# Value products of cached keys in a hybrid decoder step: three split passes with the probabilities stationary, or one fp32 pass with the values stationary

## The chip, the cores and the metric

The kernel runs on one core of one Trainium2 chip. The metric is the device time of one execution in microseconds, lower is better. Three runs of the kernel before took 2503.12 to 2511.63 us, median 2504.29 us.

## What is computed

One layer of a decoder for 512 prompt tokens and 8 x 8 sample tokens (8 sequences, 8 new tokens each) that share the weights. One projection gives queries, keys and values of 3 dilation groups x 8 heads x 128, gates, and the halves of a gated MLP. The part that the change touches is the attention of the sample tokens, over cached and over new keys:

```
kg = k_all[:, idx].astype(jnp.float32)
vg = v_all[:, idx].astype(jnp.float32)
s = jnp.einsum('bthe,btjhe->bthj', q.astype(jnp.float32), kg) * (dh ** -0.5)
s = jnp.where(valid[None, :, None, :], s, -jnp.inf)
m = jnp.max(s, axis=-1, keepdims=True)
p = jnp.exp(s - m)
den = jnp.sum(p, axis=-1)
o = jnp.einsum('bthj,btjhe->bthe', p, vg) / den[..., None]
```

The three groups' outputs are merged by their softmax denominators, which the kernel does by one softmax over all keys of all three groups. The result is multiplied by silu(z_B) and goes, with the MLP branch, through three more products and a layer norm.

## The kernel before, in words

All large products run in three passes: an operand is rounded to fp32r (the high part, ACT, L942), the rest is a second fp32r operand (the low part, VectorE, L1231, the helper low), and TensorE adds high x high, low x high and high x low.

The program has four stages: the projections of the heads (L682), then eight frames, one per head, then two products of the branches, then the output product with the layer norm. The frames run from about 1231 to 2018 us. In a frame TensorE works through 64 parts of the gates' projection (L736, six matmuls of 128x288 a part, a quarter of weights for every four parts) and between the parts does one head's attention. The order is written out by hand: 40 steps, and part_of(f, step) says behind which part a step comes (8 parts to 5 steps; in frame 1, where the attention starts later, part 16 and then 6 to 5). TensorE, ACT and VectorE each walk the same list of parts and steps, so a step's place is the same on all three, and they meet by semaphores alone.

The steps: early sample scores, four rounds of prompt scores (L792, L794), masking with maximum (L1444), exponential (L1124), normalising (L1441), turning the probabilities with transposes (L756) and prompt outputs (L804). The scores of the cached keys of two groups are made by VectorE in eight pieces, far_ones (L1419, L1420), two of them already for the next head at steps 34 and 38. At step 27 the sample probabilities are turned, and ACT copies them spread out into psh (7 tiles of 64 columns: 8 sequences x 8 tokens for each tile of 128 cached keys); VectorE makes psl, the low part.

Then come the eight value products, one per sequence b, at steps 30 to 37 (SLOT_PVS). Each needs the value tile of its sequence: 128 keys by 7 x 128 values (448 KB), which POOL's queue loads to one of four slots of cache (L559). ACT rounds it to vh (round_values, steps 24 to 36), VectorE makes vl. cached_out(b) on TensorE (L819) has the 8 probability columns of the sequence as the stationary operand and the values as the moving one, 7 tiles x 3 passes, and puts 8 rows x 128 columns to the score banks scp. At step 39 VectorE copies the 8 x 1024 results to osm (L1535); sample_out on TensorE adds up the new keys' part (L826) and turns osm back by eight transposes (L829); VectorE adds the two and multiplies by silu(z_B) in zt (L1537, L1538, L1540). That last step signals y_done.

The queues: POOL issues, in this order from a frame's end, the store of y (store_y, waits for y_done, L610), the value tiles 0 to 3 of the next head (each waits for pv_used of the product four before), the four loads of the head after it (load_head, L519 to L526), then key tiles ones 4 and 5 (L543). SP loads the gate weights (L396) and stores the gates (L403). The scores' banks are passed on by score_read, the turned probabilities' by turn_read.

Of the kernel before, what the change touches and what calls it, by code (L numbers as in the profile page):

```python
# [12 lines left out]
P = 128  # L13
# [79 lines left out]
def slot_pv(i):  # L93
# [6 lines left out]
SLOT_VS = [24, 26, 31, 32, 33, 34, 35, 36]  # L100
# [7 lines left out]
          ("pv", 2), "far", ("pv", 3), "cached_pv", "sample_out"]  # L108
N_SC = len(SCORES)
SIGNALLED = [n for n in SCORES if n != "cached_pv"]  # L110
# [28 lines left out]
def build(nc, x_t, x_res, near_k, ones_k, units_k, cache_v, w_in, bias_t, w_st, w8_t, b_s, ln_v_g, ln_v_b, w_o_a, w_o_b,  # L139
# [11 lines left out]
    with ExitStack() as ctx:  # L151
# [56 lines left out]
        far_1, far_2, otmp = put("far_1", 4, SAMP), put("far_2", SAMP), put("otmp", SAMP)  # L208
# [10 lines left out]
        place_v = R2 + 2304  # L219
        cache = put("cache", 4, 7, P)  # L220
        vl = sb("vl", [P, 4, 7, P], place_v, F32R)
# [4 lines left out]
        place_s = place_v + (28 + 56) * P * 4  # L226
        vh = [put("vh0", 7, P, dt=F32R), put("vh1", 7, P, dt=F32R)]
        sc = sb("sc", [P, 6 * P], place_s)
        pt = sb("pt", [P, 6 * P], place_s + CACHED * 4)
        place_m = place_s + 2 * CACHED * 4  # L230
        ss, psl = put("ss", KEYS + NEW), put("psl", 7 * SAMP + 4, dt=F32R)
        osm = sb("osm", [DEC_T, 8 * P], place_m)
        psh, mask = put("psh", 7 * SAMP + 4, dt=F32R), put("mask", 9 * P)
# [53 lines left out]
        ps_round, ps_zero = sem("ps_round"), sem("ps_zero")  # L287
# [4 lines left out]
        v_round, v_split, ps_split, pv_used = sem("v_round"), sem("v_split"), sem("ps_split"), sem("pv_used")  # L292
        biased, expd, normed = sem("biased"), sem("expd"), sem("normed")
        y_done, y_stored, vector_done = sem("y_done"), sem("y_stored"), sem("vector_done")
# [50 lines left out]
        def _(sp):  # L345
# [75 lines left out]
            def load_gate(n, g):  # L421

                if n >= 4:
                    sp.wait_ge(merged, n - 3)
                elif n == 0:
                    sp.wait_ge(y_done, HEADS)
                sp.wait_ge(g_stored, 16 * (g + 1))
                sp.dma_start(gbuf[:, n % 4, :], gate_d[g]).then_inc(gate_in[n % 4], 16)
# [28 lines left out]
        def _(pool):  # L457
# [150 lines left out]
            def store_y(h):  # L608
                pool.wait_ge(y_done, h + 1)
                pool.dma_start(yb_d[h], zt[h % 2]).then_inc(y_stored, 16)  # L610
            frames(frame)

            pool.wait_ge(y_done, HEADS)
# [46 lines left out]
        def _(pe):  # L660
# [84 lines left out]
            def turn_blocks(f, name, pairs_):  # L745

                n = TURN_NAMES.index(name)
                if n % 2 == 0:
                    if is_at(f, 1) and n == 0:
                        pe.wait_ge(item_read, ITEMS_ALL)  # L750
                    else:
                        pe.wait_ge(turn_read, N_TURN * (f - 1) + n)
                    if name == ("pt", 0, 0) and not is_at(f, 1):
                        pe.wait_ge(ps_split, 3 * (f - 1))
                for cols, src, rows, width in pairs_:
                    done = pe.transpose(turn[0:width, n % 2, cols:cols + rows], src, ident[0:rows, 0:rows])  # L756
                done.then_inc(turned, 1)

            def frame(f, par):
# [48 lines left out]
                def cached_out(b):  # L808
                    if b == 0:
                        bank_free("cached_pv")  # L810

                        pe.wait_ge(ps_split, 3 * f)

                    pe.wait_ge(v_split, 8 * (f - 1) + b + 1)
                    for n in range(7):
                        hi, lo = vh[b % 2][:, n, :], vl[:, b % 4, n, :]
                        at = n * SAMP + DEC_T * b
                        for t, (p, val) in enumerate(((psh, hi), (psh, lo), (psl, hi))):
                            done = pe.matmul(scp[0:DEC_T, b * P:(b + 1) * P], p[:, at:at + DEC_T], val,  # L819
                                             start=(n == 0 and t == 0), stop=(n == 6 and t == 2))  # L820
                    done.then_inc(pv_used, 1)

                def sample_out():
                    bank_free("sample_out")
                    for g in range(GROUPS):
                        pe.matmul(scp[:, SEQ:SEQ + SAMP], vN[par][g][0:SAMP, 4, :], psn[0:SAMP, g, :],  # L826
                                  start=(g == 0), stop=(g == GROUPS - 1))
                    for b in range(DEC_B):
                        done = pe.transpose(scp[:, DEC_T * b:DEC_T * (b + 1)], osm[:, b * P:(b + 1) * P],  # L829
                                            ident[0:DEC_T, 0:DEC_T])  # L830
                    done.then_inc(scored, 1)

                for part in range(PARTS):
# [11 lines left out]
                    for s in range(STEPS):  # L845
# [28 lines left out]
                        if s == 39:  # L874
                            sample_out()
# [65 lines left out]
        def _(act):  # L941
# [129 lines left out]
            def frame(f, par):  # L1071
                def turn_out(name):
# [10 lines left out]
                    elif name == ("pts", 0):  # L1083
                        probs = turn[:, bank, :]
                        copy(psh[:, 0:SAMP], probs[:, 0:SAMP]).then_inc(ps_round, 1)
                        copy(by_class(psh), probs[:, SAMP:2 * SAMP].rearrange("p (k c) -> p c k", c=4)
                             ).then_inc(ps_round, 1)
                        out = by_unit(psh)
                        src = probs[:, 2 * SAMP:3 * SAMP].rearrange("p (b u r) -> p u b r", u=2, r=4)
                    else:  # L1090
                        out, src = psn[0:SAMP], turn[0:SAMP, bank, 0:NEW].rearrange("p (n c) -> p n c", n=GROUPS)
                    copy(out, src).then_inc(turn_read, 1)

                def round_values(b):

                    slot = b % 4

                    act.wait_ge(v_in[slot], 16 * (2 * (f - 1) + b // 4 + 1))

                    if b == 0:  # L1100
                        act.wait_ge(turned, turn_no(f, ("pt", 3, 1)))
                    elif b == 1:
                        act.wait_ge(scored, signal_no(f, ("pv", 3)))
                    else:
                        act.wait_ge(pv_used, 8 * (f - 1) + b - 1)
                    copy(vh[b % 2][:], cache[:, slot, :, :]).then_inc(v_round, 1)

                for part in range(PARTS):
# [6 lines left out]
                    for s in range(STEPS):  # L1115
# [15 lines left out]
                        for b in range(DEC_B):  # L1131
                            if s == SLOT_VS[b]:
                                round_values(b)
# [5 lines left out]
            def branch_slot(t):  # L1139

                ahead(Q_B + t)
                if t == 0:
# [5 lines left out]
                    act.wait_ge(y_done, HEADS)  # L1148
# [60 lines left out]
        def _(dve):  # L1209
# [191 lines left out]
            def frame(f, par):  # L1401
# [44 lines left out]
                for part in range(PARTS):  # L1446
# [11 lines left out]
                    for s in range(STEPS):  # L1458
# [8 lines left out]
                        if s == SLOT_EARLY + 1:  # L1467
                            if f == 1:
                                dve.wait_ge(consts, 48)
                                for n_ in range(2):  # L1470
                                    dve.wait_ge(v_stored[n_], 16 * (VA_PAIRS + (2 - n_) * HEADS))
                                v.memset(psh[:].bitcast(F32), 0.0).then_inc(zeroed, 1)
# [35 lines left out]
                        if s == SLOT_FAR + 3:  # L1508
                            dve.wait_ge(expd, 5 * f)
                            normalise(ss[0:SAMP], SAMP, 5)  # L1510
                            v.memset(psl[:].bitcast(F32), 0.0).then_inc(ps_zero, 1)
                        if s == SLOT_PTS + 1:

                            b0 = TURN_NAMES.index(("pts", 0)) % 2
                            dve.wait_ge(turn_read, turn_no(f, ("pts", 1)))
                            dve.wait_ge(ps_round, 2 * f)
                            dve.wait_ge(ps_zero, f)
                            probs = turn[:, b0, :]
                            low(psl[:, 0:SAMP], probs[:, 0:SAMP], psh[:, 0:SAMP]).then_inc(ps_split, 1)
                            low(by_class(psl), probs[:, SAMP:2 * SAMP].rearrange("p (k c) -> p c k", c=4),  # L1520
                                by_class(psh)).then_inc(ps_split, 1)
                            low(by_unit(psl), probs[:, 2 * SAMP:3 * SAMP].rearrange("p (b u r) -> p u b r", u=2, r=4),
                                by_unit(psh)).then_inc(ps_split, 1)
                        for b in range(DEC_B):
                            if s == SLOT_VS[b]:

                                dve.wait_ge(v_round, 8 * (f - 1) + b + 1)
                                low(vl[:, b % 4, :, :], cache[:, b % 4, :, :], vh[b % 2][:]).then_inc(v_split, 1)
# [291 lines left out]
```

## Time and profile before

| | |
|---|---|
| median of 3 runs | 2504.29 us (2503.12 to 2511.63) |
| profiled execution, own time | 2510.55 us |
| its span, first to last instruction | 2508.9 us |
| mean granted TensorE clock | 0.965 |
| TensorE busy | 2306.7 us, 92%, 17744 records |
| VectorE busy | 1611.3 us, 64% |
| ACT busy | 923.8 us, 37% |
| POOL busy | 265.0 us, 11% |
| HBM traffic | 142 GB/s over the span |

The profile is of one execution. A matmul's end is modelled and matmuls are pipelined, so the time that one takes in a row of them is read from the distance of the starts, not from its duration. A plain fp32 matmul (and no transpose) stands in the trace as two records, each with a weight load. PE is TensorE's matmuls, PEld its weight loads. PEclk is the share of 2.4 GHz that was granted. In a matmul's row the first pair, as 128*8, is rows and columns of the stationary operand, the second, as 128x128, rows and columns of the moving one.

### The profile page before, as it was taken

To read this page: it belongs to the slowest core of one execution; us is meant where nothing else is said; L and a number is where in the kernel's file an instruction comes from. 1 tells how busy PE (TensorE), PEld (TensorE's weight loads), DVE (VectorE), ACT (ScalarE), POOL (GpSimd) and SP (SyncE) were. 2 spreads that over 40 slices of the span, in tenths; PEclk is the share of its full clock that TensorE was granted. 3 is DMA by queue.
4 is the path that set the end of the run, shared out by engine and by line. 5 is a ranking of instruction groups with operands and counts; after the bars stand their busy time and mean duration, and the time that the engine had idled before them with its cause. 6 is when DMAs were issued, how large, how long until landed. Compare 5 with 4: busy or idle time off the path is not lost.

```text
span 2508.9 us, 44550 instructions
## 1 busy us (share of the span) xinstructions
PE 2306.7 (92%) x17744; PEld 2258.8 (90%) x17744; DVE 1611.3 (64%) x2085; ACT 923.8 (37%) x1326; POOL 265.0 (11%) x453
## 2 busy tenths in 40 slices
PE   5999999999999999999968978979889979999993
PEld 4999999999999999999957978978779879999993
DVE  7677877777778777787565655655565647553336
ACT  4544444444444444444322322322323333332221
POOL 0100000000000000000222121122121110000003
PEclk8999999999999999999988999989999989999996
DMA  4433443343334333443576566566666563344332
GB/s 145 135 117 117 119 132 100 118 122 115 112 118 130 110 112 118 131 123 118 174 231 207 147 217 201 163 194 192 171 203 179 153 191 119 123 123 146 101 106 89
DMA packets 400348, 358.94 MB, mean 143 GB/s; under 512 B 15664, under 2 KB 359744, under 8 KB 398368
## 3 DMA queue, kind: packets, MB, share of 16 engines
q1 hardware_dynamic: 363168, 206.28, 28.2%
q0 software_dynamic: 36992, 149.90, 18.2%
q8 instruction: 150, 2.46, 0.4%
q14 instruction: 38, 0.31, 0.0%
HBM read 309.74 MB, written 46.37 MB: 142 GB/s over the span
## 4 chain that ended last, share of the span: by engine, by line
PE 76%; DVE 10%; DMA 7%; issue 3%; ACT 1%; POOL 1%; SPq 0%; DVEq 0%; ACTq 0%; POOLq 0%
PE acc L682 46%; PE acc L736 23%; DMA ones<-in_ones_k 4%; DVE prod L1419 2%; DVE far L1420 2%; PE scp L819 2%; PE scp L792 1%; PE turn L756 1%; DMA cache<-in_cache_v 1%; DVE sc L1444 1%; PE turn L691 1%; DMA gbuf<-gate_rows 1%; ACT wh L942 1%; DVE wl L1231 1%; DVE sc L1441 1%
## 5 line engine op out<-in xcount | busy, mean ns | idle before, releaser
L682 PE MATMUL acc<-xh,wph 128*128 128x288 f32 x2912 | 868.3, 298 | 38.4 <-DVE wpl L1231 29.2
L682 PE MATMUL acc<-xl,wph 128*128 128x288 f32 x2912 | 860.3, 295 | 0.0
L682 PE MATMUL acc<-xh,wpl 128*128 128x288 f32 x2912 | 857.2, 294 | 0.0
L682 PEld LDWEIGHTS acc<-xh,wph 128*128 128x128 f32 x2912 | 547.0, 188 | 40.9 <-issue 23.2
L682 PEld LDWEIGHTS acc<-xh,wpl 128*128 128x128 f32 x2912 | 549.5, 189 | 0.0
L682 PEld LDWEIGHTS acc<-xl,wph 128*128 128x128 f32 x2912 | 548.1, 188 | 0.0
L1231 DVE TENSOR_TENSOR wl<-raw,wh 128x512 fp32r<-128x512 f32 x256 | 176.8, 691 | 417.2 <-ACT wh L942 416.6
L942 ACT ACTIVATE wh<-raw 128x512 fp32r<-128x512 f32 x256 | 161.0, 630 | 565.6 <-PE acc L736 463.5
L736 PE MATMUL acc<-xh,wh 128*128 128x288 f32 x1024 | 237.7, 314 | 8.9 <-DVE wl L1231 6.1
L736 PE MATMUL acc<-xl,wh 128*128 128x288 f32 x1024 | 224.4, 301 | 0.0
L736 PE MATMUL acc<-xh,wl 128*128 128x288 f32 x1024 | 223.9, 301 | 0.0
L1022 ACT ACTIVATE s<-acc,bias 128x288 f32<-128x288 f32 x208 | 98.7, 500 | 273.8 <-PE acc L682 249.5
L1231 DVE TENSOR_TENSOR wpl<-w_a,wph 128x1024 fp32r<-128x1024 f32 x104 | 127.4, 1225 | 83.1 <-ACT wph L942 81.5
L736 PEld LDWEIGHTS acc<-xh,wh 128*128 128x128 f32 x1024 | 166.5, 195 | 12.5 <-DVE wl L1231 6.5
L1231 DVE TENSOR_TENSOR wpl<-w_c,wph 128x1024 fp32r<-128x1024 f32 x104 | 127.2, 1223 | 73.5 <-ACT wph L942 72.8
L736 PEld LDWEIGHTS acc<-xl,wh 128*128 128x128 f32 x1024 | 169.6, 194 | 0.0
L942 ACT ACTIVATE wph<-w_a 128x1024 fp32r<-128x1024 f32 x104 | 110.1, 1059 | 160.4 <-DVE w_a L1254 160.4
L736 PEld LDWEIGHTS acc<-xh,wl 128*128 128x128 f32 x1024 | 169.2, 194 | 0.0
L942 ACT ACTIVATE wph<-w_c 128x1024 fp32r<-128x1024 f32 x104 | 109.8, 1056 | 66.3 <-PE acc L682 63.8
L736 PE MATMUL acc<-mh,wh 128*128 128x288 f32 x512 | 110.8, 298 | 0.0
L736 PE MATMUL acc<-mh,wl 128*128 128x288 f32 x512 | 109.7, 296 | 0.0
L736 PE MATMUL acc<-ml,wh 128*128 128x288 f32 x512 | 109.5, 295 | 0.0
(212 smaller groups left out, 3637.4 us busy)
## 6 DMA issues: line engine op xcount, KB each, us to landing
raw<-in_w_in SPq DMA_DIRECT2D x128, 256.0 KB, 5.0
cache<-in_cache_v POOLq DMA_DIRECT2D x64, 448.0 KB, 5.3
w_a<-in_w_in SPq DMA_DIRECT2D x52, 512.0 KB, 3.8
w_c<-in_w_in SPq DMA_DIRECT2D x52, 512.0 KB, 3.8
w_b<-in_w_in SPq DMA_DIRECT2D x52, 512.0 KB, 3.8
w_d<-in_w_in SPq DMA_DIRECT2D x52, 512.0 KB, 3.9
ones<-in_ones_k POOLq DMA_DIRECT2D x64, 256.0 KB, 3.2
raw<-in_w_out SPq DMA_DIRECT2D x64, 256.0 KB, 2.7
```

Of the source, the lines that this page charges most:

```text
L682: done = pe.matmul(bank, w[ring][:, k, :], a[x][:, k, :], start=(j in (0, 1, 3, 5) and k == 0 and t == 0), stop=(k == HK - 1 and t == 2), ...
L691: done = pe.transpose(turn[0:rows, b, c * P:(c + 1) * P], src, ident[:])
L736: done = pe.matmul(accv[p][:, h, :], w[:, q % RING, n, :], moving(k, h, low), start=(first and n == 0 and t == 0), stop=(last and n == QB ...
L756: done = pe.transpose(turn[0:width, n % 2, cols:cols + rows], src, ident[0:rows, 0:rows])
L792: pe.matmul(scp[:, 0:SEQ], qT[par][0][:, cols], kT[par][0][:, 0:SEQ], start=True, stop=True)
L819: done = pe.matmul(scp[0:DEC_T, b * P:(b + 1) * P], p[:, at:at + DEC_T], val, start=(n == 0 and t == 0), stop=(n == 6 and t == 2))
L942: copy = lambda out, src: nc.scalar.activation(out, src, ACT.Copy)
L1022: nc.scalar.activation(out[:], bank_x, ACT.Identity, bias=b, scale=sign).then_inc(s_copied, 1)
L1231: return v.tensor_tensor(out, src, hi.bitcast(F32), ALU.subtract)
L1419: links.then(v.tensor_tensor(prod[:], keys, rows.broadcast_to([P, 4, 2, P]), ALU.mult))
L1420: v.tensor_reduce(far_1[:, :, DEC_T * b:DEC_T * b + DEC_T], prod[:].rearrange("p j u (c d) -> p j (u c) d", d=32), mybir.AxisListType.X, A ...
L1441: v.tensor_scalar(tile, tile, small[0:rows, c + 1:c + 2], None, ALU.mult).then_inc(normed, 1)
```

## The change

The value product is done in plain fp32 in one pass, with the value tile stationary (128 keys x 128 values) and the 8 probability columns moving, so that its result comes out with the values on the partitions, as the new keys' part does. It is added to that part in the same columns of the bank: the three products of the new keys (before L826) go ahead of product 0 and open the bank, and the 56 products of cached values add to it. Gone are the rounding and splitting of values (vh, vl), the splitting of probabilities (psl with its memset), osm, the eight transposes, sample_out as a step of its own, otmp and two of VectorE's three last operations. VectorE multiplies straight from the bank; it signals score_read, which takes the place of y_done everywhere. The step lists, the loads and the 64 parts are the same.

```diff
-SLOT_VS = [24, 26, 31, 32, 33, 34, 35, 36]
 SCORES = ["early", ("qk", 0), ("qk", 1), ("pv", 0), ("qk", 2), ("pv", 1), ("qk", 3),
-          ("pv", 2), "far", ("pv", 3), "cached_pv", "sample_out"]
+          ("pv", 2), "far", ("pv", 3), "sample_out"]
...
-        vh = [put("vh0", 7, P, dt=F32R), put("vh1", 7, P, dt=F32R)]
-        sc = sb("sc", [P, 6 * P], place_s)
-        pt = sb("pt", [P, 6 * P], place_s + CACHED * 4)
...
+        sc, pt = put("sc", 6 * P), put("pt", 6 * P)
+        ss, ps = put("ss", KEYS + NEW), put("ps", 7 * SAMP + 4)
...
             def store_y(h):
-                pool.wait_ge(y_done, h + 1)
+                pool.wait_ge(score_read, N_SC * (h + 1))
...
                 def cached_out(b):
                     if b == 0:
-                        bank_free("cached_pv")
-                        pe.wait_ge(ps_split, 3 * f)
-                    pe.wait_ge(v_split, 8 * (f - 1) + b + 1)
+                        bank_free("sample_out")
+                        pe.wait_ge(ps_spread, 2 * f)
+                        pe.wait_ge(turn_read, turn_no(f, ("pts", 1)))
+                        for g in range(GROUPS):
+                            pe.matmul(scp[:, SEQ:SEQ + SAMP], vN[par][g][0:SAMP, 4, :], psn[0:SAMP, g, :],
+                                      start=(g == 0), stop=False, skip_group_check=True)
+                    pe.wait_ge(v_in[b % 4], 16 * (2 * (f - 1) + b // 4 + 1))
                     for n in range(7):
-                        hi, lo = vh[b % 2][:, n, :], vl[:, b % 4, n, :]
                         at = n * SAMP + DEC_T * b
-                        for t, (p, val) in enumerate(((psh, hi), (psh, lo), (psl, hi))):
-                            done = pe.matmul(scp[0:DEC_T, b * P:(b + 1) * P], p[:, at:at + DEC_T], val,
-                                             start=(n == 0 and t == 0), stop=(n == 6 and t == 2))
+                        done = pe.matmul(scp[:, SEQ + DEC_T * b:SEQ + DEC_T * (b + 1)], cache[:, b % 4, n, :],
+                                         ps[:, at:at + DEC_T], start=False, stop=(n == 6), skip_group_check=True)
                     done.then_inc(pv_used, 1)
-
-                def sample_out():
-                    bank_free("sample_out")
-                    for g in range(GROUPS):
-                        pe.matmul(scp[:, SEQ:SEQ + SAMP], vN[par][g][0:SAMP, 4, :], psn[0:SAMP, g, :],
-                                  start=(g == 0), stop=(g == GROUPS - 1))
-                    for b in range(DEC_B):
-                        done = pe.transpose(scp[:, DEC_T * b:DEC_T * (b + 1)], osm[:, b * P:(b + 1) * P],
-                                            ident[0:DEC_T, 0:DEC_T])
-                    done.then_inc(scored, 1)
...
-                def round_values(b):
-                    slot = b % 4
-                    act.wait_ge(v_in[slot], 16 * (2 * (f - 1) + b // 4 + 1))
...
-                    copy(vh[b % 2][:], cache[:, slot, :, :]).then_inc(v_round, 1)
...
-                            v.memset(psl[:].bitcast(F32), 0.0).then_inc(ps_zero, 1)
...
-                                low(vl[:, b % 4, :, :], cache[:, b % 4, :, :], vh[b % 2][:]).then_inc(v_split, 1)
...
                         if s == 39:
                             dve.wait_ge(pv_used, 8 * f)
-                            v.tensor_copy(osm[:], scp[0:DEC_T, :]).then_inc(score_read, 1)
-                            dve.wait_ge(scored, signal_no(f, "sample_out"))
-                            links.then(v.tensor_copy(otmp[:], scp[:, SEQ:SEQ + SAMP]))
-                            v.tensor_tensor(otmp[:], otmp[:], scp[:, 0:SAMP], ALU.add).then_inc(score_read, 1)
-                            dve.wait_ge(score_read, score_no(f, "sample_out"))
-                            v.tensor_tensor(zt[par][:, SEQ:TOK], otmp[:], zt[par][:, SEQ:TOK], ALU.mult).then_inc(y_done, 1)
+                            v.tensor_tensor(zt[par][:, SEQ:TOK], scp[:, SEQ:SEQ + SAMP], zt[par][:, SEQ:TOK],
+                                            ALU.mult).then_inc(score_read, 1)
```

On TensorE in frame 2, from the last part ahead of product 0. Before, a product was 21 rows with the 8 probability columns stationary, of which the first four stand here (a matmul's size in these rows is that of its result):

```order
L736 MATMUL acc<-xh_52,wl 128x288
L736 MATMUL acc<-xh_55,wl 128x288
L819 MATMUL scp<-vh_120,psh 8x128 [waits v_split,ps_split,score_read]
L819 MATMUL scp<-vl,psh 8x128
L819 MATMUL scp<-vh_120,psl 8x128
L819 MATMUL scp<-vh_120,psh 8x128
```

Now (L728 is the old L736, L804 the old L826):

```order
L728 MATMUL acc<-xh_52,wl 128x288
L728 MATMUL acc<-xh_55,wl 128x288
L804 MATMUL scp<-psn,qkv 128x64 [waits turn_read,ps_spread,score_read]
L804 MATMUL scp<-psn,qkv 128x64 x2
L810 MATMUL scp<-ps,cache 128x8 [waits v_in0]
L810 MATMUL scp<-ps,cache 128x8 x6
L728 MATMUL acc<-xh_52,wh 128x288
```

The new keys' products have moved from behind part 62 to here, a product has 7 rows, and its first one waits for the transfer of its value tile.

On VectorE at the end of frame 2, before:

```order
L1405 COPY qz<-qkv 128x8x8 [waits head_in0,scored]
L1231 TENSOR_TENSOR wl<-raw,wh 128x512 [waits w_round]
L1419 TENSOR_TENSOR prod<-ones,qb 128x1024 [waits ones_sum,ones_in1]
L1420 TENSOR_REDUCE far_105<-prod 128x4x8 [waits vector_done]
L1535 COPY osm<-scp 8x1024 [waits pv_used]
L1537 COPY otmp<-scp 128x64 [waits scored]
L1538 TENSOR_TENSOR otmp<-otmp,scp 128x64 [waits vector_done]
L1540 TENSOR_TENSOR qkv<-otmp,qkv 128x64 [waits score_read]
```

And now (line numbers are lower by 38 and more):

```order
L1367 COPY qz<-qkv 128x8x8 [waits head_in0,scored]
L1193 TENSOR_TENSOR wl<-raw,wh 128x512 [waits w_round]
L1381 TENSOR_TENSOR prod<-ones,qb 128x1024 [waits ones_sum,ones_in1]
L1382 TENSOR_REDUCE far_105<-prod 128x4x8 [waits vector_done]
L1479 TENSOR_TENSOR qkv<-scp,qkv 128x64 [waits pv_used]
```

Four operations with a wait for TensorE between them have become one, which waits for the last value product.

## Rows read from the trace of the kernel before

**Rows 1.** The page, part 1: busy time of the engines

```profile
PE 2306.7 (92%) x17744; PEld 2258.8 (90%) x17744; DVE 1611.3 (64%) x2085; ACT 923.8 (37%) x1326; POOL 265.0 (11%) x453
```

**Rows 2.** TensorE's waits, 1230 to 2025 us: total us, times, longest us

```profile
PE turn L756 <- DVE sc L1441: 72.4, 21, 11.4
...
PE scp L826 <- DVE osm L1535: 8.5, 7, 1.3
```

**Rows 3.** The chain of waits, 1437 to 1471 us: start us, us, what

```profile
1438.70 0.64 ACT wh L942
...
1439.97 1.23 DVE prod L1419
...
1442.45 1.13 DVE osm L1535
...
1445.63 0.24 DVE qkv L1540
...
1451.97 15.04 DMA ones<-in_ones_k
```

**Rows 4.** Timeline of PE: products 0 and 7 of frame 2, and TensorE's restart

```profile
1419.89 0.22 PE L819 MATMUL scp<-vh,psh 128*8 128x128 f32 x1
...
1438.44 0.22 PE L819 MATMUL scp<-vh,psh 128*8 128x128 f32 x1
...
1470.30 1.12 PE L756 MATMUL turn<-ident,sc 128*128 128x128 f32 x4 [10.14 <-DVE sc L1441]
```

**Rows 5.** Timeline of PE: product 0 of frame 1 and the part behind it

```profile
1325.59 0.23 PE L819 MATMUL scp<-vh,psh 128*8 128x128 f32 x1
...
1326.85 0.48 PE L736 MATMUL acc<-xh,wh 128*128 128x288 f32 x2
1327.17 0.43 PE L736 MATMUL acc<-xl,wh 128*128 128x288 f32 x2
1327.44 0.43 PE L736 MATMUL acc<-xh,wl 128*128 128x288 f32 x2
```

**Rows 6.** Tile vh: count, ns least/median/most, first and last start

```profile
L819 PE MATMUL scp<-vh,psh x448: 218/223/227, 1325.6 to 2013.6; 128*8 128x128 f32 x150
...
L942 ACT ACTIVATE vh<-cache x64: 935/952/957, 1317.8 to 2009.0; 128x896 fp32r<-128x896 f32 x64
L1231 DVE TENSOR_TENSOR vl<-cache,vh x64: 1018/1092/1094, 1318.8 to 2010.0; 128x896 fp32r<-128x896 f32 x64
```

**Rows 7.** Timeline of PEld: weight loads, last one's duration 0.19, 0.14, 0.14 us

```profile
1443.62 0.74 PEld L826 LDWEIGHTS scp<-psn,qkv 64*128 64x128 f32 x6 [1.55 <-DVE osm L1535]
1444.42 0.56 PEld L829 LDWEIGHTS scp<-ident,osm 8*128 8x128 f32 x8
...
1314.67 0.54 PEld L784 LDWEIGHTS scp<-sums,far 128*64 128x64 f32 x8 [0.16 <-issue]
```

**Rows 8.** Timeline of PEld at half clock; the last load of three took 0.34 us

```profile
1375.21 0.76 PEld L794 LDWEIGHTS scp<-qkv 128*128 128x128 f32 x3 [0.52 <-issue]
...
1376.31 0.57 PEld L736 LDWEIGHTS acc<-xl,wh 128*128 128x128 f32 x2
1376.79 0.57 PEld L736 LDWEIGHTS acc<-xh,wl 128*128 128x128 f32 x2
```

**Rows 9.** The chain of waits, 1300 to 1500 us: a value tile

```profile
1421.61 6.27 DMA cache<-in_cache_v
```

**Rows 10.** Stretches: us, busy us (records) by engine, PEclk, DMA share, GB/s

```profile
1344.00:1347.40 3.40, 2.80 (x25) 2.48 (x24) 1.81 (x4) 0.00 (x0) 0.54 (x1) 1.00 0.29 77
1347.50:1350.90 3.40, 3.40 (x16) 3.40 (x16) 2.06 (x4) 1.26 (x2) 2.79 (x6) 0.50 0.53 131
1351.00:1354.30 3.30, 3.30 (x28) 3.14 (x28) 2.03 (x3) 0.63 (x1) 3.15 (x5) 1.00 0.87 275
...
1419.80:1439.80 20.00, 19.68 (x237) 18.97 (x237) 11.41 (x13) 8.33 (x11) 2.74 (x5) 1.00 0.54 174
...
1299.70:1306.40 6.70, 3.19 (x21) 2.40 (x20) 6.34 (x9) 1.55 (x4) 1.31 (x3) 1.00 0.53 164
```

More of the change, by code:

```diff
@@ L107 @@
 SCORES = ["early", ("qk", 0), ("qk", 1), ("pv", 0), ("qk", 2), ("pv", 1), ("qk", 3),
-          ("pv", 2), "far", ("pv", 3), "cached_pv", "sample_out"]
+          ("pv", 2), "far", ("pv", 3), "sample_out"]
 N_SC = len(SCORES)
-SIGNALLED = [n for n in SCORES if n != "cached_pv"]
+SIGNALLED = [n for n in SCORES if n != "sample_out"]
 N_SIG = len(SIGNALLED)
@@ L207, in build @@
         qz = put("qz", TOK)
-        far_1, far_2, otmp = put("far_1", 4, SAMP), put("far_2", SAMP), put("otmp", SAMP)
+        far_1, far_2 = put("far_1", 4, SAMP), put("far_2", SAMP)
         psn, smask, sums = put("psn", GROUPS, SAMP), put("smask", KEYS + NEW), put("sums", P)
@@ L218, in build @@
         gstage = put("gstage", TOK)
-        place_v = R2 + 2304
         cache = put("cache", 4, 7, P)
-        vl = sb("vl", [P, 4, 7, P], place_v, F32R)
         near = put("near", DEC_B * P)
@@ L225, in build @@
         ones, prod = put("ones", 2, 4 * P), put("prod", 4, 2, P)
-        place_s = place_v + (28 + 56) * P * 4
-        vh = [put("vh0", 7, P, dt=F32R), put("vh1", 7, P, dt=F32R)]
-        sc = sb("sc", [P, 6 * P], place_s)
-        pt = sb("pt", [P, 6 * P], place_s + CACHED * 4)
[L230 to L233, printed above, removed]
+        sc, pt = put("sc", 6 * P), put("pt", 6 * P)
+        ss, ps = put("ss", KEYS + NEW), put("ps", 7 * SAMP + 4)
+        mask = put("mask", 9 * P)
         m = sb("m", [P, KB, TOK], FREE)
@@ L286, in build @@
         ones_sum, units_sum, far_ready = sem("ones_sum"), sem("units_sum"), sem("far_ready")
-        ps_round, ps_zero = sem("ps_round"), sem("ps_zero")
+        ps_spread = sem("ps_spread")
         q_spread, zeroed = sem("q_spread"), sem("zeroed")
@@ L291, in build @@
         v_in = [sem(f"v_in{i}") for i in range(4)]
-        v_round, v_split, ps_split, pv_used = sem("v_round"), sem("v_split"), sem("ps_split"), sem("pv_used")
+        pv_used = sem("pv_used")
         biased, expd, normed = sem("biased"), sem("expd"), sem("normed")
-        y_done, y_stored, vector_done = sem("y_done"), sem("y_stored"), sem("vector_done")
+        y_stored, vector_done = sem("y_stored"), sem("vector_done")
         yb_in, yb_round, yb_split = sem("yb_in"), sem("yb_round"), sem("yb_split")
@@ L425, in load_gate @@
                 elif n == 0:
-                    sp.wait_ge(y_done, HEADS)
+                    sp.wait_ge(score_read, N_SC * HEADS)
                 sp.wait_ge(g_stored, 16 * (g + 1))
@@ L608, in store_y @@
             def store_y(h):
-                pool.wait_ge(y_done, h + 1)
+                pool.wait_ge(score_read, N_SC * (h + 1))
                 pool.dma_start(yb_d[h], zt[h % 2]).then_inc(y_stored, 16)
             frames(frame)
-            pool.wait_ge(y_done, HEADS)
+            pool.wait_ge(score_read, N_SC * HEADS)
             pool.dma_start(vn[:].rearrange("p c (g d) -> p c g d", g=HEADS),
@@ L752, in turn_blocks @@
                         pe.wait_ge(turn_read, N_TURN * (f - 1) + n)
-                    if name == ("pt", 0, 0) and not is_at(f, 1):
-                        pe.wait_ge(ps_split, 3 * (f - 1))
                 for cols, src, rows, width in pairs_:
@@ L873, in frame @@
                                 cached_out(b)
-                        if s == 39:
-                            sample_out()
             frames(frame)
@@ L1084, in turn_out @@
                         probs = turn[:, bank, :]
[L1085 to L1088, printed above, removed]
+                        copy(ps[:, 0:SAMP], probs[:, 0:SAMP]).then_inc(ps_spread, 1)
+                        copy(by_class(ps), probs[:, SAMP:2 * SAMP].rearrange("p (k c) -> p c k", c=4)
+                             ).then_inc(ps_spread, 1)
+                        out = by_unit(ps)
                         src = probs[:, 2 * SAMP:3 * SAMP].rearrange("p (b u r) -> p u b r", u=2, r=4)
@@ L1092, in turn_out @@
                     copy(out, src).then_inc(turn_read, 1)
-                def round_values(b):
-                    slot = b % 4
-                    act.wait_ge(v_in[slot], 16 * (2 * (f - 1) + b // 4 + 1))
[L1100 to L1105, printed above, removed]
-                    copy(vh[b % 2][:], cache[:, slot, :, :]).then_inc(v_round, 1)
                 for part in range(PARTS):
@@ L1130, in frame @@
                                                  accum_out=small[0:SAMP, 5:6]).then_inc(expd, 1)
-                        for b in range(DEC_B):
-                            if s == SLOT_VS[b]:
-                                round_values(b)
             frames(frame)
@@ L1147, in branch_slot @@
                     round_yb(6, 7, yb_raw[:, 6:7, :])
-                    act.wait_ge(y_done, HEADS)
+                    act.wait_ge(score_read, N_SC * HEADS)
                     round_yb(7, 8, zt[1].rearrange("p (o t) -> p o t", o=1))
@@ L1471, in frame @@
                                     dve.wait_ge(v_stored[n_], 16 * (VA_PAIRS + (2 - n_) * HEADS))
-                                v.memset(psh[:].bitcast(F32), 0.0).then_inc(zeroed, 1)
+                                v.memset(ps[:], 0.0).then_inc(zeroed, 1)
                             dve.wait_ge(scored, signal_no(f, "early"))
@@ L1510, in frame @@
                             normalise(ss[0:SAMP], SAMP, 5)
-                            v.memset(psl[:].bitcast(F32), 0.0).then_inc(ps_zero, 1)
[L1512 to L1527, printed above, removed]
-                                low(vl[:, b % 4, :, :], cache[:, b % 4, :, :], vh[b % 2][:]).then_inc(v_split, 1)
                         if s == 37 and f < HEADS:
```

## The prediction, made before the change was run

> **What bounds the kernel now.** I read the page first: TensorE is busy 92% of the span, every other engine far less [rows 1]. That says where to look, not what the end waits for. The waits of TensorE inside the eight frames (1230 to 2025 us) show two that repeat: 72.4 us in 21 waits for the normalised scores, and 8.5 us in 7 for the copy osm [rows 2]. The chain of waits around the end of frame 2 explains both [rows 3]. ACT's rounding starts at 1438.70, when part 59 of the frame has been multiplied. VectorE then forms two key products (1439.97 to 1442.45), copies osm, TensorE turns it back, and VectorE's last product (L1540) ends at 1445.87. Only then does POOL's queue store y and issue the next head's loads; the key tile behind them is on the way for 15.04 us. TensorE, which had work up to about 1460.2, stands idle for 10.14 us until 1470.30 [rows 4]. So a frame is a ring: y done, 24.4 us of queue, transfer and VectorE, then TensorE's parts 12 to 59, then the tail to the next y. TensorE's time counts between its restart and part 59; between y and the restart it has 10 us to spare.
>
> **The value products now.** A product is 21 matmuls of one weight load each: 1325.59 to 1326.85, 1.26 us, or 60 ns per matmul; big matmuls between them are 0.27 us apart for two, 0.133 each, and a part has six [rows 5]. In frame 2, product 0 starts at 1419.89 and product 7 at 1438.44 [rows 4]: 7 products (8.82) and 11 parts (11 x 0.80 = 8.80) make 17.62 us, and 0.9 us are waits. All 64 products are 3 x 448 matmuls [rows 6], 1344 x 0.060 = 81 us.
>
> **The new product, at full clock.** It has 7 plain fp32 matmuls with 128 value columns stationary and 8 columns moving. A plain fp32 matmul shows as two records, each with a load. The trace has no 128-wide load with 8 fp32 columns behind it, so I bound its price:
> - Nearest row: L826, a plain fp32 product, 128 stationary columns, 64 moving. Six loads take 0.74 us with one load's 0.19 us at the end, so they are (0.74 - 0.19) / 5 = 0.110 us apart [rows 7]. L784, 64 stationary and 32 moving: (0.54 - 0.14) / 7 = 0.057. Half the stationary columns, half the time: the load sets it.
> - Lower bound: the turns L829, also 128 stationary and 8 moving, (0.56 - 0.14) / 7 = 0.060 us [rows 7]. But these are transposes, another mode, with one record each.
> - Upper bound: the load at half clock, (0.76 - 0.34) / 2 = 0.21 us [rows 8].
>
> I take 0.110, because L826 is the same operation with the same load. A product becomes 14 x 0.110 = 1.54 us, 0.28 more than now. The Trainium skill, page "TensorE: Matmul & The Clock Gate", section "LDWEIGHTS (loading the stationary operand)", speaks against this change: the time of a load goes with its columns. Eight columns were loaded before and 128 now; by its formula a load of 128 is an estimated 107 ns, and the sum would be 0.04 us a product lower. The trace agrees in the pair L826 and L784.
>
> **The sum at full clock, per frame.** Up to product 7's start: seven products cost 7 x 0.28 = +1.96; the three sample products (L826) move ahead of product 0, 6 x 0.11 = +0.67; the waits there for ACT and VectorE (0.9 us in frame 2, 0.3 to 0.8 in the others, 0.5 taken) go: **+2.1 us**. The tail: part 59 ends where product 7 starts, 1438.44. VectorE's rounding and two key products stay, to 1442.45, and the one multiplication of 0.23 us follows; product 7 has ended by 1440.0 plus, so it is no wait. y is done at 1442.7 in place of 1445.87: **-3.2 us**. Together -1.1 us for frames 2 to 7; frame 1, with 8 parts instead of 11 in the stretch, about the same, a little more. In frame 8 nothing waits for y alone, but for TensorE's last part, which loses its idle 1.3 us and the eight turns but keeps the +2.1, so about +0.6. Sum: **about -7 us**, under the 0.5% (12.5 us) that a measurement of this kernel can tell from no change.
>
> **What costs or brings nothing.** ACT loses 64 copies of 0.95 us and VectorE 64 differences of 1.09 [rows 6], next to three small splits, a memset and the osm copies. They lay beside TensorE's products, and both engines wait in this stretch already, so beyond the 0.5 us above nothing comes of them. The psh copies keep their place as ps. POOL's loads wait on the same counters as before. TensorE now waits for the value tile itself: tile 4 is asked for at product 0's end and lands 6.27 us later [rows 9], 1428.9 in frame 2's terms, while product 4 is due at about 1431.5; 2.6 us to spare.
>
> **The clock.** This decides. While the old products run, the granted clock is 1.00 throughout: TensorE streams 128 columns every 60 ns, from 1419.80 to 1439.80 [rows 10]. Where did it fall? In the 3.4 us from 1344.00 TensorE was busy 2.80 us, with 25 records, 14 of them the L826 products and the 8-column turns, and the next 3.4 us ran at 0.50, that is 1.2 of 2.4 GHz. From 1299.70 it was busy only 3.19 of 6.70 us, all with long matmuls, and stayed at 1.00 [rows 10]. So short matmuls behind wide loads did not hold the clock as the long ones did, though they looked busy. The new products are of this kind: 16 columns' streaming (two records of 8) per 0.22 us of loading. Between them stand one or two parts of dense matmuls. Where two products are one part apart (steps 30/31, 32/33, 35/36) some 3.9 us hold little but loads; with two parts between them it is denser. I therefore expect three falls in each of frames 2 to 8 and five in frame 1, whose products are nearly all one part apart: 26. A fall that is not followed by a long idle lasts 3.4 us in the trace (1347.50 to 1350.90; 1.00 again after [rows 10]). In it the big matmuls take 0.24 us in place of 0.133 (0.48 for two) and loads 0.21 in place of 0.11 [rows 8], so 3.4 us do the work of 1.8: each costs 1.6 us. 26 x 1.6 = **+42 us**. All lie before part 59, on the ring. After it, a slow clock only eats the 10 us of slack.
>
> The Trainium skill (same page, Part 1, "The HAM clock gate") says the clock is released by activity and falls back without it; taken as matmul-issuing time this would keep the clock up here, and the sum would stop at -7 us. The row of 1344.00 is against that reading, so it is a rival below.
>
> **Total:** -7 + 42 = +35 us. The profiled execution took 2510.6 us, 6.3 over the median of the runs; the difference is applied to the median: 2504.3 + 35 = **2539 us**. Bounds of the clock's cost: 0, and the whole stretch at half clock.
>
> **Rivals.**
> - *The clock holds* (loads count as work): -7 us, 2497. For it: TensorE is never idle in the stretch, and in the 3.4 us before the fall at 1347.50 it was idle for 0.6. Against it: 1344.00. Chance 0.20.
> - *Faster, the other side: the load goes at the turns' pace*, 0.060 us instead of 0.110, in L810 of the change. Then a product takes 0.84 us, -0.42; a stretch 7 x -0.42 + 0.67 - 0.5 = -2.8, the tail -3.2, so -6.0 in seven frames and -4 in the last: -46 us, 2458. It decides from a spacing below about 0.085 us, where a product is cheaper than the old 1.26. For: same load width, same 8 moving columns. Against: L826. Chance 0.08.
> - *The clock stays at half from product 0 to part 59*, because one dense part between products does not bring it back. The stretch of 0.67 + 10.8 + 8.8 = 20.3 us takes 1.3 + 7 x 3.0 + 11 x 1.44 = 38 us: +18 a frame, +144 - 7 = +137, 2641. For: after the stall at 1470 it needs dense work to return. Against: two-part gaps are over half dense. Chance 0.10.
> - *Value tiles land late*: some 1 to 2 us a frame on top, 2550. Chance 0.05.
> - My forecast: 0.57, with 2515 to 2590 as its own range.
>
> **The numbers.** Range 2494 to 2590: it leaves out the fast load and the full half clock. Faster by over 0.5% takes the fast load and the low edge of the first rival: 0.12. Within 0.5%: the rest of that rival and a few falls only: 0.22. Slower: 0.66.
>
> **What would show it.** L810: 896 records about 0.110 us apart at full clock and 0.21 at half; product 0 to product 7 20.3 us where the clock is 1.00 throughout; half-clock stretches of 3.4 us inside the product stretches; VectorE's single product about 4.2 us after product 7's start; no wait for osm; the 24.4 us from y to TensorE's restart unchanged. A spacing of 0.06, or a clock of 1.00 in all eight stretches, would prove the forecast wrong.

## The result, and the profile after

The changed kernel takes 2588.65 us (median of 4 runs, 2568.40 to 2600.82) against 2506.67 before (4 runs): a ratio of 1.032, 95% interval 1.025 to 1.039. It is slower, by 82 us, where 35 were forecast. The time lies 1.4 us under the upper edge of the range (2590), and two of the four executions lie above that edge, so it is luck that the median fell inside. The profiled execution took 2590.81 us, against 2510.55 before.

The page of the changed kernel, part 1, to be read beside [rows 1]:

```profile
PE 2400.2 (93%) x17232; PEld 2357.0 (91%) x17232; DVE 1522.9 (59%) x1965; ACT 864.5 (33%) x1262; POOL 264.1 (10%) x453
```

TensorE has 512 records fewer and is busy 94 us longer. ACT and VectorE have lost 59 and 88 us of work; the end did not come sooner for it. TensorE's waits, as in [rows 2]:

```profile
PE turn L746 <- DVE sc L1403: 69.1, 21, 9.8
```

The wait for osm is gone; the large one, for the normalised scores after each frame's start, has kept its size. No wait for a value tile is in the list. So the 82 us are not a wait: TensorE works through the frames more slowly. The timeline of PEld in frame 3 shows how:

```profile
1538.02 1.75 PEld L810 LDWEIGHTS scp<-ps,cache 128*128 128x128 f32 x14
1539.65 0.55 PEld L728 LDWEIGHTS acc<-xh,wh 128*128 128x128 f32 x2
...
1541.07 3.13 PEld L810 LDWEIGHTS scp<-ps,cache 128*128 128x128 f32 x14
```

A product of 14 loads takes 1.6 us at full clock and 3.0 at half; the clock fell at the end of the first one. Big matmuls start 0.24 us apart (0.48 for two). The price of a load is 0.112 us from start to start at full clock and 0.213 at half (medians over the records of all 64 products at that clock): the forecast had 0.110 and 0.21.

The stretches from product 0 to product 7's start, all eight frames; the columns are those of [rows 10], PEclk is the last but two:

```profile
1328.90:1359.40 30.50, 30.50 (x147) 30.50 (x147) 6.19 (x7) 1.26 (x2) 2.73 (x5) 0.54 0.29 87
1436.50:1460.80 24.30, 24.30 (x165) 24.30 (x165) 3.84 (x5) 1.26 (x2) 2.72 (x5) 0.79 0.47 142
1538.00:1570.60 32.60, 32.60 (x165) 32.58 (x165) 3.84 (x5) 1.26 (x2) 2.72 (x5) 0.58 0.34 106
1648.50:1676.10 27.60, 27.60 (x165) 27.57 (x165) 3.84 (x5) 1.26 (x2) 2.72 (x5) 0.69 0.40 125
1753.10:1785.70 32.60, 32.60 (x165) 32.60 (x165) 3.84 (x5) 1.26 (x2) 2.72 (x5) 0.57 0.35 106
1863.40:1890.90 27.50, 27.50 (x166) 27.50 (x166) 3.84 (x5) 1.26 (x2) 2.72 (x5) 0.69 0.41 126
1968.10:2000.80 32.70, 32.70 (x167) 32.66 (x166) 3.84 (x5) 1.26 (x2) 2.72 (x5) 0.57 0.34 106
2071.20:2095.40 24.20, 24.20 (x166) 24.20 (x166) 1.38 (x2) 1.26 (x2) 2.19 (x4) 0.80 0.45 132
```

Together 232.0 us, where the kernel before took 143.2 for the same eight (16.3 to 18.6 each, at 1.00 throughout). A mean clock of 0.57 over 32.6 us means 2 x (1 - 0.57) x 32.6 = 28 us at half clock. In all it is 165 us. Below, a "fall" is a piece of time at half clock. In frames 1, 3, 5 and 7 the clock fell with the first product or two and stayed down almost to the last: one fall of 34.1 us in frame 1, which runs on past product 7, and of 23.9 us in the others. In the even frames it rose in between: frames 2 and 8 have three falls of 3.4 us each, frames 4 and 6 have one of 10.2 us among them. Two pieces of frame 2 and one of frame 3, in the same columns:

```profile
1440.60:1443.80 3.20, 3.20 (x15) 3.20 (x15) 0.00 (x0) 0.09 (x1) 0.55 (x1) 0.50 0.72 220
1444.10:1447.20 3.10, 3.10 (x29) 3.10 (x28) 2.80 (x3) 0.24 (x1) 0.54 (x1) 1.00 0.36 109
1539.60:1563.30 23.70, 23.70 (x106) 23.70 (x106) 3.49 (x4) 1.26 (x2) 2.72 (x5) 0.50 0.39 122
```

The account closes on starts of instructions. Product 7 of frame 8 starts at 2012.56 before and at 2095.36 now, +82.8 us. Of it +3.3 lie ahead of frame 1's product 0, +88.8 in the eight stretches, and -9.3 in the seven pieces from a product 7 to the next frame's product 0 (543.7 before, 534.5 now; 1.3 us a frame). The chain of waits at the end of frame 2, beside [rows 3]:

```profile
1461.14 0.64 ACT wh L921
...
1462.41 1.23 DVE prod L1381
...
1463.67 1.23 DVE far L1382
...
1465.18 0.53 POOL ones L535
1465.71 3.36 DMA yb_rows<-qkv
...
1472.18 14.14 DMA ones<-in_ones_k
...
1489.61 0.47 PE turn L746
```

From product 7's start (1460.85) to the end of y are 4.16 us, against 7.43 before, as the tail was forecast; to the store of y they are 4.86 us, against 7.71. The store has lost a little less than y itself, because the load of a key tile (1465.18) now goes out immediately ahead of it (before, that load started at 1442.74 and the store at 1446.16). POOL's queue then waits for the store to land, 3.36 us, and sends the head's first load 3.64 us behind the store, against 2.98 before (1446.16 to 1449.14). In this frame the restart of TensorE comes 23.9 us behind the store, against 24.1; in the mean of frames 1 to 6 it is 24.6 against 24.1, in single frames between 1.7 us less and 1.6 us more than before. The stall itself is still there, 9.70 us in this frame.

### The profile page after: what moved, and what is told of

The parts are those of the page before. It is cut to its first block, busy times and chain, and to the rows that moved or that the text cites. A ratio compares the mean times of both kernels' runs of the same rounds, so it can differ in the third digit from the quotient of the medians.

```text
span 2589.1 us, 43270 instructions
## 1 busy us (share of the span) xinstructions
PE 2400.2 (93%) x17232; PEld 2357.0 (91%) x17232; DVE 1522.9 (59%) x1965; ACT 864.5 (33%) x1262; POOL 264.1 (10%) x453
## 3 DMA queue, kind: packets, MB, share of 16 engines
q0 software_dynamic: 36992, 149.90, 17.8%
## 4 chain that ended last, share of the span: by engine, by line
PE 80%; DVE 9%; DMA 6%; issue 2%; ACT 1%; POOL 1%; SPq 0%; DVEq 0%; ACTq 0%; POOLq 0%
PE acc L674 44%; PE acc L728 26%; PE scp L810 5%; DMA ones<-in_ones_k 2%; DVE prod L1381 2%; DVE far L1382 2%; DMA raw<-in_w_in 2%; PE scp L782 1%; PE turn L746 1%; DVE sc L1406 1%; DMA gbuf<-gate_rows 1%; PE turn L683 1%; ACT wh L921 1%; DVE wl L1193 1%; DVE sc L1403 1%
## 5 line engine op out<-in xcount | busy, mean ns | idle before, releaser
L728 PE MATMUL acc<-xh,wh 128*128 128x288 f32 x1024 | 258.7, 337 | 9.9 <-DVE wl L1193 7.1
L728 PE MATMUL acc<-xl,wh 128*128 128x288 f32 x1024 | 240.4, 319 | 0.0
L728 PE MATMUL acc<-xh,wl 128*128 128x288 f32 x1024 | 239.7, 318 | 0.0
L728 PEld LDWEIGHTS acc<-xh,wh 128*128 128x128 f32 x1024 | 183.5, 214 | 13.3 <-DVE wl L1193 7.5
L728 PEld LDWEIGHTS acc<-xl,wh 128*128 128x128 f32 x1024 | 185.8, 212 | 0.0
L728 PEld LDWEIGHTS acc<-xh,wl 128*128 128x128 f32 x1024 | 184.6, 211 | 0.0
L810 PEld LDWEIGHTS scp<-ps,cache 128*128 128x128 f32 x896 | 148.2, 254 | 0.5
L810 PE MATMUL scp<-ps,cache 128*128 128x8 f32 x896 | 143.0, 295 | 0.0
L728 PE MATMUL acc<-mh,wh 128*128 128x288 f32 x512 | 110.8, 298 | 0.0
```

What stands on the lines that cost most here:

```text
L728: done = pe.matmul(accv[p][:, h, :], w[:, q % RING, n, :], moving(k, h, low), start=(first and n == 0 and t == 0), stop=(last and n == QB ...
L810: done = pe.matmul(scp[:, SEQ + DEC_T * b:SEQ + DEC_T * (b + 1)], cache[:, b % 4, n, :], ps[:, at:at + DEC_T], start=False, stop=(n == 6), ...
```

## Experiments

Times are medians; the ratio is to runs of the kernel before in the same job. Rivals are numbered as in the expectations.

**Same loads, 64 columns moved.** Diff to the changed kernel:

```diff
-                        done = pe.matmul(scp[:, SEQ + DEC_T * b:SEQ + DEC_T * (b + 1)], cache[:, b % 4, n, :],
-                                         ps[:, at:at + DEC_T], start=False, stop=(n == 6), skip_group_check=True)
+                        first = DEC_T * b // 64 * 64
+                        done = pe.matmul(scp[:, SAMP * b + first:SAMP * b + first + 64], cache[:, b % 4, n, :],
+                                         ps[:, n * SAMP + first:n * SAMP + first + 64], start=(n == 0), stop=(n == 6))
```

VectorE then copies the new keys' part to otmp, adds the 8 x 8 wanted columns and multiplies, three operations instead of one.

> The change, but each value product moves all 64 probability columns of a tile (all eight sequences) in place of its own 8, into a bank of its own per sequence; VectorE picks the 8 that are wanted and adds the new keys' part. Loads, their number and their width are the same. My theory (what moves behind the load decides the clock; the load decides the spacing): spacing stays 0.112 us, the granted clock stays 1.00 in all eight product stretches, product 0 to product 7 takes 20 to 21 us, the time is 2500 to 2518 us. Rival 1 (wide fp32 loads lower the clock, whatever moves): half-clock stretches as in the changed kernel, 2575 to 2605 us. Rival 2 (the spacing is not the load's): spacing over 0.13 us and a time in between.

2511.48 us (10 runs), ratio 1.0027 (1.0017 to 1.0037). Spacing 0.112 us again. Three of its stretches (frames 1, 2 and 8):

```profile
1329.30:1346.80 17.50, 17.50 (x149) 17.46 (x148) 4.51 (x6) 1.26 (x2) 2.73 (x5) 1.00 0.48 151
1422.80:1442.60 19.80, 19.80 (x165) 19.78 (x165) 3.84 (x5) 1.26 (x2) 2.72 (x5) 1.00 0.57 175
...
1992.90:2012.80 19.90, 19.90 (x166) 19.83 (x166) 1.40 (x3) 1.26 (x2) 2.19 (x4) 1.00 0.51 161
```

The clock is 1.00 in all eight, and they take 156.1 us together (17.4 in frame 1, 19.8 in each of the others, a little less than the 20 to 21 expected). The same loads in the same number and places, with eight times the columns behind each, cost no more time, and 76 of the 89 us are gone. That settles the main question for this kernel: the spacing is the same with 8 and with 64 columns behind each load, and the clock is not. Rivals 1 and 2 fall.

**32 columns.** The same with 32 for 64.

> The same with 32 moving columns, those of four sequences. My theory: spacing 0.112 us again, the clock falls in some of the stretches but for shorter than with 8, 2515 to 2570 us. Rival 1 (loads): as the changed kernel, 2575 to 2605 us.

2510.21 us (10 runs), ratio 1.0013 (1.0002 to 1.0024). Here I was wrong: the clock held in all eight stretches, 156.1 us again. The forecast time, 2515 us and more, was missed by 5 us. Half the columns are as good as all.

**16 columns.**

> As the kernel with 64 moving columns, with 16, those of two sequences. With 64 and with 32 the clock stayed at 1.00 in all product stretches. If what moves per load decides, 16 is nearer to 8: half-clock stretches in the products again, fewer or shorter than the changed kernel's 165 us, 2515 to 2580 us. If 8 columns is a case of its own (a smallest size), none, about 2510 us.

2576.64 us (4 runs, 2562.70 to 2586.12), ratio 1.026 (1.023 to 1.029). Of its stretches, those of frames 2, 4 and 6:

```profile
1428.70:1459.50 30.80, 30.80 (x166) 30.80 (x166) 3.84 (x5) 1.26 (x2) 2.72 (x5) 0.61 0.37 112
...
1642.30:1663.20 20.90, 20.90 (x166) 20.89 (x166) 3.84 (x5) 1.26 (x2) 2.72 (x5) 0.94 0.54 165
...
1846.80:1879.20 32.40, 32.40 (x166) 32.36 (x165) 3.84 (x5) 1.26 (x2) 2.72 (x5) 0.58 0.35 107
```

All eight take 233.0 us, as with 8 columns, with 167 us at half clock against 165 (the profiled execution is the slowest of the four). The time lies in the expected range, but the falls are neither fewer nor shorter than with 8. So 8 is no case of its own. No gradual change shows: 8 and 16 columns cost alike, 32 and 64 cost nothing; no number between 16 and 32 was run. The same program gives, frame by frame, 20.9 to 32.4 us in frames 2 to 8. This run is built as those with 64 and 32 columns are, with the new keys' part kept apart and three operations on VectorE, and it falls all the same; so it was the columns, and nothing else in that form, that held the clock there.

**One pass, the old way round.** The kernel before with unsplit operands; the rounding, the splits and psl are taken out:

```diff
-                        hi, lo = vh[b % 2][:, n, :], vl[:, b % 4, n, :]
                         at = n * SAMP + DEC_T * b
-                        for t, (p, val) in enumerate(((psh, hi), (psh, lo), (psl, hi))):
-                            done = pe.matmul(scp[0:DEC_T, b * P:(b + 1) * P], p[:, at:at + DEC_T], val,
-                                             start=(n == 0 and t == 0), stop=(n == 6 and t == 2))
+                        done = pe.matmul(scp[0:DEC_T, b * P:(b + 1) * P], ps[:, at:at + DEC_T], cache[:, b % 4, n, :],
+                                         start=(n == 0), stop=(n == 6))
```

> Only the one-pass half of the change: values and probabilities in plain fp32, no splitting, but the 8 probability columns stationary and the 128 value columns moving, with osm and the turning back as before. My theory: two records of 0.109 us per product matmul, a product 1.53 us against 1.26, the clock at 1.00 in all stretches, and the old tail of 7.4 us from product 7 to y; +1.3 to +1.9 us a frame, 2510 to 2522 us. Rival 1 (wide loads): also no falls here, so it only tells that the orientation, not plain fp32, brings the falls. Rival 3 (plain fp32 in one pass lowers the clock): 2575 us and more.

2530.39 us (4 runs), ratio 1.010 (1.008 to 1.012). No fall in any stretch, and 0.109 us a record, as expected, so rival 3 (plain fp32 in one pass lowers the clock) falls too; but the time is 8 us over the range. A stretch takes 21.5 us where 7 x 1.53 + 8.8 = 19.5 were worked out. The trace of tile ps gives the rest:

```profile
L810 PEld LDWEIGHTS scp<-cache,ps x896: 85/90/91, 1326.0 to 2034.0; 128*8 128x8 f32 x180
...
  issue: 10.4, 64
```

Ahead of each of the 64 products TensorE stands still for 0.16 us, and behind it the next two big matmuls start 0.20 and 0.24 us apart instead of 0.13: some 0.3 us a product for the change between this form and the big products. In the change's form there is no such cost (19.8 us for 19.6 worked out). So plain fp32 in one pass, whichever way round, is dearer at full clock than the three fp32r passes of the kernel before (14 x 0.109 or 14 x 0.112 against 21 x 0.060). The falls do not come with plain fp32 as such: this way round, with 128 columns moving behind each load, there are none.

**Products farther apart.**

```diff
-SLOT_PVS = [30, 31, 32, 33, 34, 35, 36, 37]
+SLOT_PVS = [28, 29, 31, 32, 34, 35, 37, 38]
```

> The changed kernel with its eight products at steps 28, 29, 31, 32, 34, 35, 37 and 38: with frames 2 to 8 two or three dense parts between any two but the last pair, in place of one or two. Same instructions. If the falls come from products that stand close together, the half-clock time in the product stretches drops well below 165 us and the time to 2520 to 2570 us; frame 1, still close, keeps its fall. If the falls come from the loads as such, or from the number of products, no change: 2575 to 2605 us.

2518.14 us (10 runs, 2508.80 to 2529.91), ratio 1.004 (1.002 to 1.006). Frames 1, 2, 3 and 6:

```profile
1326.40:1359.60 33.20, 33.20 (x172) 33.20 (x172) 6.63 (x8) 1.89 (x3) 2.73 (x5) 0.59 0.31 96
1431.70:1455.40 23.70, 23.70 (x195) 23.70 (x195) 5.93 (x8) 3.15 (x5) 2.73 (x5) 1.00 0.48 147
1529.90:1555.20 25.30, 25.30 (x195) 25.30 (x195) 5.96 (x8) 3.16 (x5) 2.74 (x5) 0.93 0.43 137
...
1820.50:1849.00 28.50, 28.50 (x197) 28.50 (x196) 6.02 (x8) 3.15 (x5) 2.73 (x5) 0.82 0.40 122
```

The half-clock time in the stretches goes from 165 to 44 us, 27 of them in frame 1, where the products still stand close, and this is the slowest of the ten executions. Frames 2, 4, 5 and 8 have none; 3, 6 and 7 still have 3.4, 10.2 and 3.4 us, so spreading makes the falls rarer and does not rule them out. The time is 2 us better than the expected 2520. The same instructions in other places give back 70 of the 82 us: the falls come from products close together, as the forecast said.

**The ring, on the kernel before.**

```diff
-                if f < HEADS:
-                    if h > 0:
-                        pool.wait_ge(y_stored, 16 * h)
-                    load_head(f, 1 - par)
                 load_ones(h, 4)
                 load_ones(h, 5)
+                if f < HEADS:
+                    if h > 0:
+                        pool.wait_ge(y_stored, 16 * h)
+                    load_head(f, 1 - par)
```

> The kernel before, with POOL issuing key tiles 4 and 5 ahead of the next head's four loads. It tests the ring: if a frame's start hangs on y, queue and transfer, with TensorE idle 8 to 11 us, then the key tile lands some 7 us sooner in frames 2 to 7, TensorE restarts that much sooner, 2450 to 2475 us. Rival (TensorE's work sets the frame): no change, 2500 to 2508 us. A third way: the head's loads come late for step 37 and give it back.

2456.18 us (4 runs), ratio 0.981 (0.979 to 0.983). The restart of frame 3 in its timeline of PE:

```profile
1449.64 0.55 PE L756 MATMUL turn<-ident,sc 128*128 128x128 f32 x3 [2.07 <-DVE sc L1441]
```

The idle time there is 2.07 us, after 10.14 in [rows 4]. From the store of y to the restart it is 17.8 us in the mean of frames 1 to 6, after 24.1: the ring is real, and 6 of its 24 us hung on two loads' place in the queue. This version beats both kernels, by 50 and 130 us.

**Both: 32 columns and that order.**

> 32 moving columns (clock held) together with POOL's order with key tiles 4 and 5 ahead of the head's loads. On the kernel before that order gave 2456 us and left TensorE 2 us of waiting per frame, so TensorE's own work sets the frame there. The one-pass product adds 1.6 us a frame to the stretch and 0.7 ahead of it, and takes away from the end the 1.3 us of waiting for osm, 0.7 of sample products and 0.6 of turns: about -0.3 a frame. Expected 2448 to 2462 us. Rival (the longer stretch counts in full, the end nothing): 2470 to 2476 us.

2473.78 us (4 runs), ratio 0.987 (0.986 to 0.989): 18 us slower than that order on the kernel before. I was wrong, and the rival's number came true. So did most of its account. Product 7 of frame 8 starts 20.0 us later than in the run of that order alone (1977.42 against 1957.46); 13.9 us of that lie in the eight stretches (156.1 against 142.2), 1.7 ahead of frame 1's product 0, and 4.4 in the seven pieces between. The longer stretch counts in full, and the shorter tail brings nothing. Why it brings nothing the rival did not say. The chain of waits at the end of frame 2:

```profile
1432.57 0.34 SPq L395
...
1432.95 12.12 DMA raw<-in_w_in
...
1445.10 0.64 ACT wh L921
```

A quarter of the gate weights, asked for at 1432.9, takes 12.12 us, and TensorE stands idle 3 to 8 us at the frame's start, against 2 to 3. POOL has sent four value tiles from 1432.07 on, 0.9 us ahead of that quarter. In the run of that order alone a quarter that was asked for 1.6 us behind the value tiles took 9.6 us. So my reading is that the shorter tail brought the big loads closer to the weights' own; no run moved the one without the other, and it is not shown.

**The change and that order.**

> The changed kernel, 8 columns, with POOL's new order. Falls of the clock as in the changed kernel cost 76 us in the stretches; with less slack after them the slow clock behind part 59 costs too: 2530 to 2560 us. If the order of the loads had been part of the loss, it would come below 2510 us.

2546.52 us (4 runs), ratio 1.016 (1.013 to 1.019), as expected: the falls come back with 8 columns (221.8 us in the stretches, 143 at half clock), and the time is 73 us over the run with 32. Here the long falls lie in frames 1, 5, 6 and 7.

## Why the prediction was right, and where it was off

- *The ring* was read rightly: the stall kept its size, time in the stretches counted in full, and the order of loads moved the end by 50 us.
- *The price of a load*, 0.110 us taken from L826: measured 0.112. The argument for it, L826 against L784 (0.110 and 0.057), did not settle that the load sets the pace, since the moving columns halve there too, 64 and 32; the runs with 8 to 64 moving columns behind the same load, all at 0.112, do. The rival of a load at the turns' pace (0.060) is out. That those are transposes does not explain their pace: the transposes of L756, 128x128, start 0.109 us apart at full clock. Why the small ones are faster stays open.
- *The stretch at full clock*, +2.1 us with the sample products: by the run with 64 columns 19.8 against 18.1 in the mean of frames 2 to 8, +1.7, and 0.8 for the sample products ahead of it, +2.5.
- *The tail*, -3.2 us: measured -3.3 from product 7 to the end of y in frame 2, and -2.8 to the store of y in the mean of frames 2 to 7. The load of a key tile just ahead of the store was not foreseen, and in the mean of frames 1 to 6 another 0.5 us came back between the store and the restart; that the one is the cause of the other was not tested. The full-clock sum of -7 us is measured, by the ratios with 32 and 64 columns, as +3 and +7 us: nothing gained. The extra VectorE work in those runs explains little of it: y ends 0.5 us later, but its store comes only 0.08 us later (4.94 against 4.86 us behind product 7).
- *The clock* was the step that decided, and its mechanism held: short movements behind wide loads, close together, let it fall. **Mis-sized was the term of +42 us**: "26 x 1.6", falls of 3.4 us, which makes 88 us at half clock. It measured 165 us at half clock and 76 us of cost (232.0 less 156.1). The price of a microsecond at half clock was right, 0.46 us against 1.6 / 3.4 = 0.47; the length of the falls was not. I took it from the trace of before, where dense matmuls followed the fall and the clock was up again at once. In frames 2 and 8 it came so, three falls of 3.4 us each. In the others loads went on and falls joined, to 10.2, 23.9 or 34.1 us. That is the rival "stays at half from product 0 to part 59", which nearly came true in four frames of eight (28 of 30.5 to 32.6 us at half clock; it had 38 us for a stretch). It should have stood in the forecast as a share, not beside it. The forecast's own sign, falls of 3.4 us inside the stretches, holds for two frames alone.

Two more things stay open. Why odd frames stay down and even ones recover in this execution is not explained; the executions differ by 32 us (2568 to 2601), and with the other order of loads other frames stay down, so it is hardly a fixed pattern. And why the old way round in fp32 costs 0.3 us at each change of form was seen, not tested.

## What to carry to other kernels

A matmul with a wide stationary operand and a few moving columns can be paid twice, as here: the load sets its pace (0.11 us for 128 fp32 columns here, 0.21 at half clock), and a run of them can drop TensorE's clock for everything around. Look at the granted clock of the stretch, not at the busy share, which was 100% at half speed. Then either move more columns behind each load (here 32 cost no more than 8 and held the clock) or spread such products between dense ones. And before shortening an engine's work, find out what it waits for at the stage's start: moving two loads in a queue brought 50 us where the whole redesign brought none.

## What the runs showed of the hardware

- Plain fp32 records with 128 stationary columns start 0.112 us apart with 8, 16, 32 or 64 moving columns at full clock.
- The clock held at 1.00 in all eight stretches with 32 moving columns, and fell in all eight with 16: the time is 2510 us with 32 and 2577 us with 16. The Trainium skill, page "TensorE: Matmul & The Clock Gate", Part 1, says that activity releases the clock. In the changed kernel's stretches TensorE's records filled 100% of the time, and the granted clock was 0.54 to 0.80 all the same.
- The same eight products gave falls of different length from frame to frame: at most 3.4 us in frames 2 and 8, 10.2 in 4 and 6, 23.9 in 3, 5 and 7, 34.1 in frame 1.
- Over all eight stretches a microsecond at half clock cost 0.46 us (76 us for 165).
- A 256 KB load of weights that took a median of 5.0 us took 12.12 us when it was asked for 0.9 us behind four value tiles of 448 KB, and 9.6 us in another run, 1.6 us behind them.
